# Experts of 128 slots with rounded weights become experts of 96 slots in f32, on four column quarters of TensorE

## The chip, the cores and the metric

The kernel runs on one core of a Trainium2 chip. The metric is the device time of one execution in microseconds, the median of several. The profile is one more execution; all its times are counted from the start of its span.

## The reference

One inference step of a decoder layer: a recurrent branch and an attention branch, merged and projected, and then a mixture of experts over 520 tokens (512 of the prompt, 8 of the samples). The change is in the mixture:

```python
D_MODEL = 1024; N_EXPERTS = 32; TOP_K = 4; D_FF = D_MODEL
logits = (t @ router_w).astype(jnp.float32) + router_b
top_v, top_e = lax.top_k(logits, TOP_K)
gate = jax.nn.softmax(top_v, axis=-1)
# for each expert e, for the tokens that chose it:
#   up = t @ w_up[e] + b_up[e]            (1024 -> 2048: a gate half and a linear half)
#   h  = clamped SwiGLU of the two halves (limit 7)
#   y += gate * (h @ w_down[e] + b_down[e])
```

An expert's weights are 1024 x 2048 and 1024 x 1024 f32 numbers: 12 MB, of which each number is used once for each of the 65 tokens (520 x 4 / 32) that an expert has on average. All 32 experts are read from HBM: 402.7 MB.

## The kernel before, in words

Up to about 650 us the kernel computes the branches, the projection and the router. The experts follow; they are sorted by their token counts, so that those with few tokens take the small places in a fixed pattern of places. The loops have a fixed number of steps and each place has a fixed number of slots (rows): 128 in 21 places and 64 (`FEW`) in 11. Places 0 and 1 have 128; then `triple` runs nine times with one place of 64 and two of 128; then `pair` and a last place of 64.

Weights come in 12 pieces of 1 MB for each expert: chunks 0 to 3 are the up matrix (512 columns each), 4 and 5 the down matrix, each in two halves. SyncE issues them (L612) into a ring in SBUF that holds 12 pieces, one expert. A piece is issued when the semaphore `half_used` says that the piece that lay there has been used, and TensorE counts `half_used` up behind the last matmul of each half.

A place of 128 slots (`block_of`) multiplies with f32 numbers split into two rounded parts (fp32r): for each product there are three matmuls, high x high, high x low, low x high. ScalarE makes the high part of each weight piece (`high_half`, L1846, a copy from the ring into one of six buffers `WH`), VectorE makes the low part (`low_half`, L2631, a subtraction in place in the ring), and both are needed before TensorE may start on the piece (L1350 up, L1367 down). Rows and hidden values are split the same way (L1888, L2707, L1896, L2726).

A place of 64 slots (`few_block`) multiplies in plain f32, straight from the ring, with nothing for ScalarE and VectorE to split. Its 64 rows use half of the array's columns, so each product is two matmuls side by side, one on columns 0 to 63 and one on columns 64 to 127, each with half of the 512 weight columns (L1403; in the down matrix L1418, of 512 of the 1024 columns each). Each f32 matmul of the program that is no transpose stands in the trace as two MATMUL and two LDWEIGHTS records (704 such products in `few_up` are the 1408 records of L1403); a rounded one and a transpose as one of each.

Around that, GpSimd gathers the rows of the next place (L2923) and adds the finished rows to the output in HBM (L2933), both with indirect DMAs; TensorE transposes the gathered rows (L1296, L1303) and the hidden values (L1315, L1411) by matmuls with the identity; biases are bf16 matmuls (L1319, L1396); ScalarE applies the gelu (L1892, L1940) and scales the results (L1935, L1963); VectorE clamps and multiplies (L2719, L2722, L2772, L2775).

## Time and profile before

| | |
|---|---|
| median of 3 runs | 1739.96 us (1731.2 to 1741.41) |
| span of the profiled execution | 1731.7 us |
| TensorE matmuls busy | 1665.8 us, 96% |
| VectorE busy | 1137.0 us, 66% |
| ScalarE busy | 888.9 us, 51% |
| read from HBM, written | 488.10 MB, 25.35 MB |

The profile's page divides the span into 40 slices of 43.3 us; each digit is the busy share of the slice in tenths. PE is TensorE's matmuls, PEld its weight loads, DVE VectorE, ACT ScalarE, POOL GpSimd, SP SyncE; "SPq" and "ACTq" are the queues of instructions of these engines. In a row of the timeline the columns are start, length, engine, line, operation, output<-input, shapes, and the count of merged instructions; in brackets stands idle time before them and what ended it.

### The profile page before, as it was taken

To read this page: it belongs to the slowest core of one execution; us is meant where nothing else is said; L and a number is where in the kernel's file an instruction comes from. 1 tells how busy PE (TensorE), PEld (TensorE's weight loads), DVE (VectorE), ACT (ScalarE), POOL (GpSimd) and SP (SyncE) were. 2 spreads that over 40 slices of the span, in tenths; PEclk is the share of its full clock that TensorE was granted. 3 is DMA by queue.
4 is the path that set the end of the run, shared out by engine and by line. 5 is a ranking of instruction groups with operands and counts; after the bars stand their busy time and mean duration, and the time that the engine had idled before them with its cause. 6 is when DMAs were issued, how large, how long until landed. Compare 5 with 4: busy or idle time off the path is not lost.

```text
span 1731.7 us, 27748 instructions
## 1 busy us (share of the span) xinstructions
PE 1665.8 (96%) x10106; PEld 1295.3 (75%) x10106; DVE 1137.0 (66%) x1555; ACT 888.9 (51%) x1019; POOL 217.4 (13%) x260
## 2 busy tenths in 40 slices
PE   7999999999998999999999999999989999999998
PEld 4899988798777777767677686767768676776765
DVE  6866785655356868949385684939477593938661
ACT  5245655533423446647274664728375573727461
POOL 0022000003331033110001001001000101100100
PEclk9999999999999999999999999999999999999999
DMA  5063233114437329999999999999999999999996
GB/s 219 30 215 120 84 123 101 46 62 134 140 107 261 104 71 403 348 396 402 398 405 378 409 386 398 394 399 399 384 410 383 400 397 403 395 395 409 381 399 231
DMA packets 100436, 498.74 MB, mean 288 GB/s; under 512 B 16350, under 2 KB 33846, under 8 KB 49648
## 3 DMA queue, kind: packets, MB, share of 16 engines
q1 hardware_dynamic: 84288, 458.39, 67.3%
q0 software_dynamic: 15920, 38.71, 7.9%
q8 instruction: 50, 0.82, 0.2%
q10 hardware_dynamic: 144, 0.55, 0.1%
q14 instruction: 34, 0.28, 0.0%
HBM read 488.10 MB, written 25.35 MB: 297 GB/s over the span
## 4 chain that ended last, share of the span: by engine, by line
PE 73%; DMA 14%; DVE 7%; issue 3%; ACT 2%; POOL 0%; ACTq 0%; SPq 0%; DVEq 0%; POOLq 0%
DMA ring<-in_w_exp 13%; PE bank L1350 13%; PE bank L1367 12%; PE bank L1403 9%; PE bank L795 7%; PE bank L695 5%; PE bank L850 5%; PE bank L1418 4%; PE bank L722 3%; PE bank L1114 2%; DVE ring_rounded L2631 1%; PE bank L662 1%; PE bank L863 1%; PE bank L884 1%; PE bank L872 1%
## 5 line engine op out<-in xcount | busy, mean ns | idle before, releaser
L2631 DVE TENSOR_TENSOR ring_rounded<-ring,wide_rounded 128x2048 fp32r<-128x2048 f32 x126 | 283.7, 2285 | 21.5 <-ACT wide_rounded L1846 21.3
L1846 ACT ACTIVATE wide_rounded<-ring 128x2048 fp32r<-128x2048 f32 x126 | 236.6, 1912 | 86.4 <-DMA ring<-in_w_exp 72.6
L1350 PE MATMUL bank<-ring_rounded,slab_rounded 128*128 128x512 f32 x672 | 264.3, 394 | 0.0
L1350 PE MATMUL bank<-xn_rounded,slab_rounded 128*128 128x512 f32 x672 | 224.9, 407 | 1.2 <-DVE ring_rounded L2631 0.8
L2631 DVE TENSOR_TENSOR ring_rounded<-ring,xn_rounded 128x2048 fp32r<-128x2048 f32 x84 | 190.2, 2285 | 20.6 <-ACT xn_rounded L1846 19.2
L1367 PE MATMUL bank<-wide_rounded,slab_rounded 128*128 128x512 f32 x504 | 172.4, 403 | 9.3 <-DVE slab_rounded L2726 8.9
L1846 ACT ACTIVATE xn_rounded<-ring 128x2048 fp32r<-128x2048 f32 x84 | 159.5, 1909 | 22.8 <-DMA ring<-in_w_exp 19.3
L2772 DVE TENSOR_SCALAR slab<-bank 128x256 f32<-128x256 f32 x22 | 9.3, 424 | 237.6 <-PE bank L1403 237.6
L1350 PE MATMUL bank<-wide_rounded,slab_rounded 128*128 128x512 f32 x504 | 159.0, 390 | 0.0
L1403 PE MATMUL bank<-ring,slab 128*64 128x256 f32 x1408 | 156.2, 380 | 0.0
L1350 PEld LDWEIGHTS bank<-xn_rounded,slab_rounded 128*128 128x128 f32 x672 | 130.0, 193 | 33.5 <-ACT xn_rounded L1846 3.4
L795 PE MATMUL bank<-ring_rounded 128*128 128x260 f32 x768 | 147.7, 291 | 0.0
L1350 PEld LDWEIGHTS bank<-ring_rounded,slab_rounded 128*128 128x128 f32 x672 | 128.2, 191 | 26.0
L2933 POOL DMA_INDIRECT out_y<-slab,small x32 | 58.5, 1828 | 674.2 <-ACT slab L1935 364.0
L1403 PEld LDWEIGHTS bank<-ring,slab 128*64 128x64 f32 x1408 | 98.1, 137 | 51.2 <-issue 1.9
L1367 PE MATMUL bank<-ring_rounded,slab_rounded 128*128 128x512 f32 x336 | 131.7, 392 | 0.0
L795 PEld LDWEIGHTS bank<-ring_rounded 128*128 128x128 f32 x768 | 117.8, 188 | 14.0 <-issue 11.9
L1367 PEld LDWEIGHTS bank<-wide_rounded,slab_rounded 128*128 128x128 f32 x504 | 95.3, 189 | 32.8 <-issue 13.2
L1350 PEld LDWEIGHTS bank<-wide_rounded,slab_rounded 128*128 128x128 f32 x504 | 94.7, 188 | 19.5
L2631 DVE TENSOR_TENSOR ring_rounded<-ring,qT_rounded 128x2048 fp32r<-128x2048 f32 x42 | 95.9, 2283 | 0.0
L695 PE MATMUL bank<-ring_rounded 128*128 128x260 f32 x512 | 93.6, 285 | 0.8 <-ACT wide L1534 0.8
L1846 ACT ACTIVATE qT_rounded<-ring 128x2048 fp32r<-128x2048 f32 x42 | 80.3, 1912 | 2.3 <-DMA out_y<-slab 2.3
(553 smaller groups left out, 2988.2 us busy)
## 6 DMA issues: line engine op xcount, KB each, us to landing
ring<-in_w_exp SPq DMA_DIRECT2D x384, 1024.0 KB, 14.0
ring<-in_w_blk SPq DMA_DIRECT2D x40, 512.0 KB, 3.3
slab<-in_w_tok SPq DMA_DIRECT2D x4, 1304.0 KB, 15.0
ring<-in_w SPq DMA_DIRECT2D x8, 512.0 KB, 3.3
ring<-in_w_out SPq DMA_DIRECT2D x2, 2048.0 KB, 15.5
xn<-in_xT SPq DMA_DIRECT2D x4, 520.0 KB, 7.9
ring<-in_k_cmp SPq DMA_DIRECT2D x32, 64.0 KB, 3.5
ring<-in_k_cmp POOLq DMA_DIRECT2D x32, 64.0 KB, 2.6
```

What stands on the lines that cost most here:

```text
L695: r = mm(bank[:, banks + h, 0:HN], w[:, k, wcols], a[:, k, cols], start=first and x == 0, stop=last and x == 2)
L722: r = mm(out, u[:, k, q], w[:, k, a:b], start=k == 0 and x == 0, stop=k == KD - 1 and x == 2)
L795: r = mm(bank[:, 6 + h, 0:HN], w[:, k, :], a[:, k, cols], start=k == 0 and y == 0, stop=k == KD - 1 and y == 2)
L850: r = mm(bank[:, 4 * h + 2 * f + x, :].rearrange("p (g c) -> p g c", g=NPAGES), w[:, f, x, :], a, start=l == 0 and y == 0, stop=l == LP - ...
L1114: return mm(out, three[0][x][k][:, a:a + n], w[:, k, :], start=first, stop=last)
L1350: r = mm(bank[:, c, :], a[:, 4 * h + k, :], w[:, k, :], start=False, stop=h == 1 and i == 11)
L1367: r = mm(bank[:, 4 + y, :], a[:, k, :], w[:, f, cols], start=k == 0 and x == 0, stop=k == KD - 1 and x == 2)
L1403: r = mm(bank[FEW * h:FEW * h + FEW, c, 0:256], XF[:, k, :], w[:, k, 256 * h:256 * h + 256], start=False, stop=k == KD - 1)
L1418: r = mm(bank[FEW * y:FEW * y + FEW, 4, :], HF[:, 2 * (c - 4) + k % 2, k // 2, :], w[:, k, y * 512:(y + 1) * 512], start=c == 4 and k == 0 ...
L1846: fn(WH[(2 * c + h) % 6], ring[:, half_of(c, h)], ACT.Copy).then_inc(S["wh_ready"], 1)
L2631: v.tensor_tensor(ring_r[:, half_of(c, h)], ring[:, half_of(c, h)], WHf[(2 * c + h) % 6], ALU.subtract)\
L2933: pool.indirect_dma_start(out=d["y"][:, :], out_offset=bass.IndirectOffsetOnAxis(ap=index, axis=0), in_=rows, in_offset=None, bounds_check ...
```

## The change

All places now work in plain f32. There are three kinds: 96 slots (`MID`, 20 places), 64 slots (`FEW`, 11 places, as before, save that the down matrix goes by 512 columns too), and one of 128 slots (`WIDE_AT`, place 14). The order of the places is written out as a list; the loop body is a group of six places, run twice, then the wide place, then the group twice again, then five places by themselves. A place of 96 slots has its three groups of 32 rows on three quarters of the array's columns, each with weight columns 0 to 383; the fourth quarter does weight columns 384 to 511 for all three groups, one after the other.

The splitting instructions of ScalarE and VectorE and their buffers are gone, and with them the semaphores `wh_ready`, `wl_ready`, `xl_ready` and `hl_ready`. TensorE waits for each 1 MB piece by itself (`piece_in`). The order of the pieces of the down matrix is (4,0), (5,0), (4,1), (5,1), and in HBM each of them is four blocks of 128 rows by 512 columns. VectorE gets one more small copy for each place (the gates of the rows that stand in the fourth quarter, or in the upper half), and ScalarE scales a place of 96 slots with eight instructions in place of one. The rows of the next place are transposed behind the first hidden part, before the down matrix.

```diff
-FEW = 64
-TRIPLES = 9
+FEW, MID = 64, 96
+GROUP = (MID, FEW, MID, MID, FEW, MID)
+BEFORE, BEHIND = 2, 2
+WIDE_AT = 2 + len(GROUP) * BEFORE
+LAST = (MID, FEW, MID, FEW, FEW)
+CAP = (MID, MID) + GROUP * BEFORE + (P,) + GROUP * BEHIND + LAST
...
+        PIECE_ORDER = [(c, h) for c in range(4) for h in range(2)] + [(4, 0), (5, 0), (4, 1), (5, 1)]
...
+            def product(c, slots, rows, w, first, last):
+                if slots == P:
+                    return mm(bank[:, c, :], rows(0, P), w, start=first, stop=last)
+                if slots == FEW:
+                    for y in range(2):
+                        r = mm(bank[64 * y:64 * y + 64, c, 0:256], rows(0, 64), w[:, 256 * y:256 * y + 256], start=first, stop=last)
+                    return r
+                for g in range(3):
+                    mm(bank[32 * g:32 * g + 32, c, 0:384], rows(32 * g, 32), w[:, 0:384], start=first, stop=last)
+                for g in range(3):
+                    r = mm(bank[96:128, c, P * g:P * (g + 1)], rows(32 * g, 32), w[:, 384:512],
+                           start=first and g == 0, stop=last and g == 2)
+                return r
...
+            def up_half(n, c, h, slots):
+                pe.wait_ge(piece_in[2 * c + h], 16 * n + 32)
+                w = weights(c, h)
+                for k in range(4):
+                    r = product(c, slots, lambda a, m: XT[:, 4 * h + k, a:a + m], w[:, k, :], False, h + k == 4)
+                r.then_inc(S["half_used"], 1)
...
+            def down(n, slots, meanwhile=None):
+                turn_hidden(n, slots, 0)
+                if meanwhile is not None:
+                    meanwhile()
+                pe.wait_ge(S["y_scaled"], n + 1)
+                pe.wait_ge(S["hh_ready"], 2 * n + 1)
+                down_half(n, 4, 0, slots)
+                turn_hidden(n, slots, 1)
+                down_half(n, 5, 0, slots)
                 pe.wait_ge(S["hh_ready"], 2 * n + 2)
+                down_half(n, 4, 1, slots)
+                down_half(n, 5, 1, slots)
...
-                fn(WH[(2 * c + h) % 6], ring[:, half_of(c, h)], ACT.Copy).then_inc(S["wh_ready"], 1)
...
-                v.tensor_tensor(ring_r[:, half_of(c, h)], ring[:, half_of(c, h)], WHf[(2 * c + h) % 6], ALU.subtract)\
-                    .then_inc(S["wl_ready"], 1)
```

On TensorE, at the start of the second place of `triple` before (chunk 0 of 128 slots): the biases and the first products, each row a run of equal matmuls with the shape of its output.

```order
L1319 MATMUL bank<-oT,kT 128x512 x4
L1339 ISA
L1350 MATMUL bank<-xn_rounded,slab_rounded 128x512
L1350 MATMUL bank<-ring_rounded,slab_rounded 128x512
L1350 MATMUL bank<-xn_rounded,slab_rounded 128x512 x2
L1350 MATMUL bank<-ring_rounded,slab_rounded 128x512
```

On TensorE now, in the first place of the group of six (96 slots): the end of the up matrix, the transposes, and the start of the down matrix.

```order
L1323 MATMUL bank<-ring,slab 32x384 x3
L1325 MATMUL bank<-ring,slab 32x128 x3
L1377 REGISTER_ALU
L1379 MATMUL bank<-ident,slab 128x128 x3
L1309 REGISTER_ALU
L1312 MATMUL bank<-ident,slab 128x128
L1312 MATMUL bank<-ident,slab 128x64 x7
L1343 REGISTER_ALU
L1323 MATMUL bank<-ring,slab 32x384 x3
L1325 MATMUL bank<-ring,slab 32x128 x3
```

Where three matmuls of 512 columns on the whole array stood for one block of 128 weight rows, six f32 matmuls on quarters stand now, 48 times six for each place.

On VectorE, in a place of 128 slots before: two of the subtractions stand between the hidden values' instructions, and a place has twelve.

```order
L2631 TENSOR_TENSOR ring_rounded<-ring,wide_rounded 128x2048
L2726 TENSOR_TENSOR slab_rounded<-bank,slab_rounded 128x512
L2631 TENSOR_TENSOR ring_rounded<-ring,wide_rounded 128x2048
L2718 REGISTER_ALU
L2719 TENSOR_SCALAR slab<-bank 128x512
L2720 REGISTER_ALU
L2722 SCALAR_TENSOR_TENSOR slab<-slab 128x512
```

On VectorE now, a place of 96 slots whole, behind the copies for the place before it:

```order
L2597 CAST kT<-small 96x128
L2589 COPY small<-small 128x1
L2594 COPY qT<-qT 32x3
L2602 TENSOR_SCALAR slab<-bank 128x384
L2605 SCALAR_TENSOR_TENSOR slab<-slab 128x384
```

The subtractions are gone, and only the hidden values' instructions and three small copies are left.

## Rows read from the trace of the kernel before

**Rows 1.** The page: busy time, then 40 slices; in it TensorE, DMA share, GB/s
```profile
PE 1665.8 (96%) x10106; PEld 1295.3 (75%) x10106; DVE 1137.0 (66%) x1555; ACT 888.9 (51%) x1019; POOL 217.4 (13%) x260
PE   7999999999998999999999999999989999999998
DMA  5063233114437329999999999999999999999996
GB/s 219 30 215 120 84 123 101 46 62 134 140 107 261 104 71 403 348 396 402 398 405 378 409 386 398 394 399 399 384 410 383 400 397 403 395 395 409 381 399 231
```

**Rows 2.** Stretches: length, engines' busy time (count), clock, DMA share, GB/s
```profile
843.70:943.00 99.30, 96.61 (x512) 71.27 (x510) 66.01 (x48) 56.42 (x44) 9.53 (x6) 0.98 1.00 396
700.00:740.00 40.00, 39.75 (x187) 32.10 (x186) 37.30 (x33) 25.33 (x18) 4.83 (x2) 1.00 0.93 341
906.00:961.00 55.00, 55.00 (x329) 40.87 (x329) 28.63 (x25) 22.17 (x21) 5.62 (x4) 1.00 0.98 383
961.00:976.00 15.00, 14.74 (x67) 9.01 (x64) 11.40 (x6) 12.62 (x9) 1.95 (x2) 1.00 1.02 425
1702.00:1717.00 15.00, 15.00 (x142) 9.53 (x140) 1.13 (x4) 2.20 (x4) 1.56 (x1) 1.00 0.70 262
```

**Rows 3.** DMA queues from 850 to 1640 us: packets, MB, share of 16 engines
```profile
q0 software_dynamic: 5888, 13.04, 6.5%
q14 instruction: 1, 0.01, 0.0%
```

**Rows 4.** SyncE's queue: who it waited for, in total, times, longest
```profile
SPq L612 <- PE bank L1350: 421.5, 168, 14.1
```

**Rows 5.** The page's groups: the splitting of one kind of piece
```profile
L2631 DVE TENSOR_TENSOR ring_rounded<-ring,wide_rounded 128x2048 fp32r<-128x2048 f32 x126 | 283.7, 2285 | 21.5 <-ACT wide_rounded L1846 21.3
L1846 ACT ACTIVATE wide_rounded<-ring 128x2048 fp32r<-128x2048 f32 x126 | 236.6, 1912 | 86.4 <-DMA ring<-in_w_exp 72.6
```

**Rows 6.** Timeline of TensorE, one place of 64 slots
```profile
843.51 0.63 PE L1396 MATMUL bank<-oT,kT 96*64 96x256 bf16 x8
843.97 10.53 PE L1403 MATMUL bank<-ring,slab 128*64 128x256 f32 x96
...
860.39 1.04 PE L1296 MATMUL bank<-ident,slab 128*128 128x128 f32 x8
...
866.66 1.04 PE L1319 MATMUL bank<-oT,kT 96*128 96x512 bf16 x4
```

**Rows 7.** Timeline of TensorE: f32 matmuls of 32 rows on four quarters
```profile
522.95 3.64 PE L996 MATMUL bank<-ring,wide 128*32 128x512 f32 x32
...
542.09 1.95 PE L1080 MATMUL bank<-slab,kT 128*32 128x128 f32 x64
543.86 2.58 PE L1080 MATMUL bank<-ring,kT 128*32 128x128 f32 x88
548.69 1.51 PE L1080 MATMUL bank<-ring,kT 128*32 128x128 f32 x40 [2.24 <-issue]
```

**Rows 8.** DMA queue of TensorE's code, in 0 to 520 us
```profile
q8 instruction: 28, 0.46, 0.4%
```

**Rows 9.** The same stretch, as a row of stretches
```profile
0.00:520.00 520.00, 503.42 (x3521) 433.48 (x3522) 334.69 (x764) 235.62 (x451) 76.19 (x147) 1.00 0.35 115
```

**Rows 10.** DMA queues in 541 to 546 us, then in 546 to 549 us
```profile
q1 hardware_dynamic: 137, 1.98, 93.1%
...
q8 instruction: 1, 0.02, 2.2%
```

**Rows 11.** Timeline of the end: last piece issued, last matmuls, scaling, last add
```profile
1702.01 0.33 SPq L612 DMA_DIRECT2D ring<-in_w_exp  x1
...
1718.75 5.37 PE L1418 MATMUL bank<-ring,slab 128*64 128x512 f32 x24
...
1724.25 1.38 ACT L1963 ACTIVATE slab<-bank,small 64x512 f32<-64x512 f32 x2 [5.01 <-PE bank L1418]
1726.53 1.44 POOL L2933 DMA_INDIRECT out_y<-slab,small  x1 [20.78 <-ACT slab L1963]
```

**Rows 12.** Pieces issued after 1690 us, from issue to landing
```profile
DMA to landing us min/median/max: 11.1/14.6/15.3
```

More of the change, by code:

```diff
@@ L196, in build @@
         eslot = [0, 1, 2, 4, 3, 5]
-        ebase = [16 * loads[s] for s in eslot]
         def chunk(name, n=1):
@@ new lines, in block_of, with groups @@
+            def block_of(n, b, slots, following, by_column=True):
+                gated(n, slots, 0)
+                gated(n, slots, 1)
+                hidden_copied(n, slots, 0)
+                if following:
+                    turned_rows(n + 1, following)
+                hidden_copied(n, slots, 1)
+                scaled(n, b, slots, by_column)
+            def groups(count, first, following):
+                with act.Fori(0, count) as t:
+                    for i, slots in enumerate(GROUP):
+                        block_of(len(GROUP) * t + (first + i), (first + i) % 2, slots, (GROUP + (following,))[i + 1])
@@ L2801, in _, with groups @@
+            def groups(count, first):
+                with dve.Fori(0, count) as t:
+                    for i, slots in enumerate(GROUP):
+                        block_of(len(GROUP) * t + (first + i), (first + i) % 2, slots, True)
             pick_expert(0, pick_two)
@@ L2803, in _ @@
             places(RT - 1)
-            low_rows(0)
             gate_low(RT - 1)
```

581 lines of the change are left out of this document (187 added, 394 removed).

## The prediction

> **What bounds the kernel now.** I read the page's slices first [rows 1]. TensorE is at 9 tenths almost everywhere, and from slice 16 (650 us) on the DMA engines are at 9 tenths too, at some 395 GB/s. So the 1060 us of experts have two candidates. The stretches tell them apart [rows 2]. One triple (two places of 128 slots, one of 64) lasts 99.3 us, 33.1 us an expert; TensorE's matmuls are busy 96.6 of it and the DMA share is 1.00. Inside it the load is uneven: right behind the place of 64 slots (961 to 976 us) the engines move 425 GB/s, and through the second place of 128 slots and the one of 64 (906 to 961 us) 383 GB/s at a share of 0.98, with TensorE busy all 55 us and SyncE's queue waiting for it to give pieces back: 421.5 us in 168 waits for L1350 alone [rows 4]. Each bounds in turn: TensorE while it is on large places, the DMA behind a small one.
>
> At 425 GB/s a piece of 1.049 MB takes 2.47 us, twelve take 29.6 us. The indirect gathers and adds take 6.5% of the engines [rows 3], 2.15 us of 33.1. With some code packets beside them (2.2% of 3 us x 16 engines is 1.06 us of one engine each [rows 10], five for an expert 0.3 us) the DMA floor is 32.1 us an expert, 1.0 us under today's pace. That 1.0 us is what a TensorE with slack can free; how fast it is beyond that does not matter.
>
> VectorE (66 of 99.3 us) and ScalarE (56) have slack already, so the work that goes away there, 12 subtractions of 2.285 us and 12 copies of 1.912 us for each large place [rows 5], is worth only the waits that it causes: the 2.7 us of a triple in which TensorE is not busy.
>
> **The change, part by part.** *A place of 96 slots.* Its shape is not in the trace, its parts are: on four quarters at once 32 records of 128x512 take 3.64 us with a last one of 0.59 us unhidden in part, 8 rounds of 0.43 us; and of 128x128, 88 records take 2.58 us, 22 rounds of 0.109 us [rows 7]. So four quarters do run side by side in f32, and a round costs its columns. For one block of 128 weight rows, three quarters have two records of 384 columns, 2 x 0.32 = 0.64 us, the fourth has six of 128, 6 x 0.109 = 0.656 us. The larger counts: 48 x 0.656 = 31.5 us. Biases: four banks of 0.16 us. Transposes: 6 hidden and 8 of rows at about 0.11 us (8 take 1.04 with the tail [rows 6]), 1.5 us. Six switches between whole and quartered array at 0.1 to 0.2 us, 1 us. Sum 34.7 us. Bounds: 33.5 us if the fourth quarter costs no more than the others, 40 us if its six loads leave gaps of a sixth.
>
> *A place of 64 slots.* Its products are the same matmuls in halves of 256 columns; it lasted 23.2 us (843.5 to 866.7) [rows 6]. I keep that.
>
> *The wide place.* 48 products of 512 columns at two records of 0.43 us [rows 7], 41.2 us, with the rest 44. It costs its neighbours 44 - 32 = 12 us at most, once; the small place three before it and the ring's twelve pieces hide part. I take 5 us.
>
> *Per three experts* TensorE then needs 2 x 34.7 + 23.2 = 92.6 us, against 96.3 us at the DMA floor. It keeps 3.7 us of slack, so the DMA sets the pace. Two large places in a row need 69.4 us where the DMA would give 64.2; the ring (12 pieces) covers the 5.2 us. I take 32.4 us an expert, a little above the floor, because there will be such pairs. From 740 to 1700 us are 29 experts: 29 x (33.1 - 32.4) = -20 us, bounds 0 and -29; with the wide place -15.
>
> *The start.* Expert 0's pieces come at the same events of the router. In 700 to 740 us the DMA share is 0.93 [rows 2], since TensorE gave pieces back late, behind the first splits: -3 us, bounds 0 and -8.
>
> *The end.* The last piece is issued at 1702.0 us, because a large place held it [rows 11], and lands at the latest 15.3 us later [rows 12]; from 1702 to 1717 us the share is 0.70 [rows 2]. With pieces free early the engines stay full: -4.5 us. From 1717.3 us to TensorE's last matmul, 1724.1 us, are 6.8 us of work on pieces that lie there; a TensorE that waits for pieces has only the last one to do, four blocks of four records in pairs, 8 rounds of 10.53 / 48 = 0.219 us [rows 6], 1.75 us: -5 us. Scaling and the add behind it stay (7.6 us), bounds 0 and -10 for both.
>
> *Waits that are new.* TensorE waits for `piece_in` with the next matmuls queued behind it; that is the DMA's pace, priced above. It waits for `hh_ready` behind the transposes of the first hidden part; the eight row transposes stand between (8 x 0.109 = 0.87 us), and ScalarE's copy of 384 columns is shorter than the 512 columns that it scales in 1.38 / 2 = 0.69 us [rows 11]. ScalarE's eight scalings, 2.5 us by estimate (eight at under half of 0.69), are waited for at the next place's down matrix, 22 us later. Cover everywhere; without it 1 us a place.
>
> *Code.* In 0 to 520 us TensorE ran 3521 matmuls and 3522 loads [rows 9] and its code queue brought 28 packets of 16 KB [rows 8]: one packet for 251 instructions. In 850 to 1640 us, eight triples, it brought none [rows 3]: the loop body, some 1000 instructions, stays where it was read. The new body is four places of about 1230 (288 x 4 and 76) and two of 420, 5760 instructions; I count on it being read again all the time, one packet for 128 matmuls, which last 128/12 x 0.656 = 7.0 us. The trace has one place where code was late: the fast run of L1080 stops after 64 + 88 matmuls for 2.24 us with nothing awaited [rows 7], and the packet came in 546 to 549 us, not while the DMA was 93% busy before [rows 10]. 128 matmuls back is the 24th of the first run, at 542.8 us; the stop ends at 548.7. So a packet was usable 5.9 us after the one before it was entered, under a nearly full DMA. 5.9 is under 7.0: hidden, with 1.1 us to spare.
>
> By the Trainium skill (Runtime: NRT & Kernel Launch, Instruction fetch mechanics), TensorE's instruction memory holds 2048 instructions and is refilled in blocks of 256 while the current block runs. The trace agrees with the block (251) and with a body of 1000 that stays; that 5760 do not stay is that page's word, no row of this kernel shows it.
>
> **Sum.** -15 - 3 - 4.5 - 5 = -27.5 us. The profiled execution's 1731.7 us becomes 1704; it lies 8.3 us under the median of the runs, and on that scale 1740 - 27.5 = 1712 us, -1.6%.
>
> **Rivals.** *1. Code arrives too late (slower).* If a packet takes 9 us instead of 5.9 (the DMA share here is 1.02, not 0.93), a large place takes 1230/256 x 9 = 43 us, three experts 109.6 us, 36.5 an expert: 29 x 3.4 = +99, less some 7 of start and end, 1832 us. It decides from 7.9 us a packet: then a large place takes 38.1 and three experts 99.3 as now. For it: one late packet in a busy stretch. Against: if TensorE falls back, fewer pieces are in flight and packets come sooner, which pulls towards 8.5 us, 1786 us. 23%.
>
> *2. It comes out even.* Packets of 7.5 to 8 us, or a fourth quarter with gaps, so that a large place takes 36.5 to 38 us: the pace stays 33 us, only part of the ends is gained, 1723 to 1757 us. 20%.
>
> *3. The quarters do not overlap when unequal.* If the fourth quarter's six records ran behind the others instead of beside them, a block would take 1.3 us, a large place 65 us: 20 x 30 = +600 us, 2300 us. Against: no round of four in rows 7 costs more than its columns, though all are equal there. 3%.
>
> *4. Records cost a fixed time.* Twelve records for a block leave 55 ns each. In rows 7 88 records take 2.58 us, 27 ns each after the tail, so 12 need 0.33 us at least and the block's 0.656 is not touched. Were a whole load and matmul paid in turn, 2 x 27 = 54 ns for each record, it would still be 0.65 us. Only at a cost of 62 ns or more would it bind: 0.74 us a block, a large place 38.9 us, three experts 101 us, +16 - 7, 1749 us. 2%.
>
> By the Trainium skill (TensorE: Matmul & The Clock Gate, Wait — 56ns, not 53.3ns?) a matmul can cost about 62 ns in the sequencer. By the 27 ns of rows 7 this trace denies it.
>
> **Numbers.** The forecast, DMA-bound at 32.1 to 32.9 us an expert, gives 1690 to 1722 us: 52%. Faster by over 1% (1% is about what a measurement of this kernel can tell from no change; under 1722.6) 0.52, within 1% 0.20, slower 0.28 (rivals 1, 3, 4). Range: down to 1692 (all of the pace, 29, and all of the ends), up to 1786 (rival 1 at 8.5 us).
>
> **What would show it.** Right: a group of six places of about 194 us at 425 GB/s outside the gathers; TensorE idle in short waits for pieces, in small places above all; 0.66 us for each block in a large place; code packets every 7 us in large places and no idle time there marked "issue"; the last matmul less than 3 us behind the last landing. Wrong: idle time of TensorE of 1 to 3 us each 128 matmuls with landed pieces in the ring; DMA share under 0.97 in the pace; blocks of over 0.75 us.

## The result, and the profile of the changed kernel

The changed kernel takes 1747.32 us (median of 4, 1745.54 to 1754.53) against 1736.55 us of the kernel before (1731.20 to 1741.41): a ratio of 1.0078, with a 95% interval of 1.0045 to 1.0111. It is slower by 0.8%, where 1.6% faster was forecast. The profiled execution's span is 1744.4 us, 12.7 more than 1731.7.

The page: busy time of the engines, and three of the rows of 40 slices, as in [rows 1].

```profile
PE 1652.3 (95%) x19416; PEld 1401.3 (80%) x19416; DVE 521.3 (30%) x1271; ACT 466.1 (27%) x930; POOL 194.1 (11%) x263
PE   7999999999999999999998998999998899999896
DMA  5064233124547239999999999999999999999995
GB/s 215 32 218 119 79 123 109 37 66 128 145 124 269 69 112 394 361 378 389 405 393 402 397 398 405 398 372 371 392 403 390 384 374 404 387 405 400 390 410 230
```

VectorE fell from 1137 to 521 us and ScalarE from 889 to 466, as the edit says. The bytes per microsecond hardly moved (393 GB/s against 396 from 850 to 1640 us): the splitting went away and the DMA engines deliver what they delivered.

Stretches, with the columns of [rows 2]: about the first and the second round of the first group of six places, the place of 128 slots, 33 us behind the second jump back, and the last pieces.

```profile
740.00:940.00 200.00, 193.05 (x3056) 172.32 (x3060) 14.47 (x42) 36.39 (x79) 17.12 (x14) 0.99 1.01 395
940.00:1138.00 198.00, 187.14 (x2857) 163.43 (x2850) 14.47 (x42) 30.93 (x66) 12.25 (x10) 0.99 1.01 398
1138.00:1182.00 44.00, 43.93 (x121) 20.06 (x123) 2.96 (x6) 5.54 (x10) 2.44 (x2) 1.00 0.98 368
1378.00:1411.00 33.00, 30.43 (x467) 28.14 (x467) 2.59 (x7) 2.07 (x4) 0.48 (x1) 0.82 0.95 361
1711.00:1735.00 24.00, 18.52 (x152) 10.34 (x148) 1.92 (x6) 1.66 (x5) 0.00 (x0) 1.00 0.57 227
```

TensorE now has slack (187 of 198 us), the DMA share is 1.01, and 395 to 398 GB/s is within 1% of the 396 GB/s of the triple in [rows 2]. The DMA queues from 850 to 1640 us, as in [rows 3]:

```profile
q1 hardware_dynamic: 40636, 295.92, 93.4%
q0 software_dynamic: 4862, 12.93, 6.7%
q8 instruction: 89, 1.46, 0.7%
```

And the same stretch's row of weights in the kernel before:

```profile
q1 hardware_dynamic: 41191, 299.94, 94.4%
```

In the same 790 us 4 MB of weights fewer arrive than before, and 1.46 MB of code do arrive, where there was none. From the start of place 1 to that of place 31 (found by the bf16 bias matmuls) the kernel before takes 989.7 us, the changed one 993.7. Counted by the DMA instead (an expert has landed when the last of its 1536 weight packets of 8 KB has ended), the landings of experts 1 to 30 span 963.6 us before and 977.4 now, and the last expert takes 41.0 us more, 36.0 before. Places in which TensorE does not wait are as forecast: 34.1 to 34.4 us for 96 slots, 23.1 for 64, 44.0 for 128.

The inside of a place of 96 slots, as in [rows 7]: one block of 128 weight rows is two such pairs of rows.

```profile
740.72 0.50 PE L1323 MATMUL bank<-ring,slab 128*32 128x384 f32 x3
740.74 0.49 PE L1325 MATMUL bank<-ring,slab 128*32 128x128 f32 x3
741.04 0.50 PE L1323 MATMUL bank<-ring,slab 128*32 128x384 f32 x3
741.07 0.49 PE L1325 MATMUL bank<-ring,slab 128*32 128x128 f32 x3
```

The three quarters' records start every 0.32 us and the fourth's run beside them: 0.65 us a block, with 0.656 in the sum. What TensorE waited for in 740 to 1700 us (total, times, longest):

```profile
PE bank L1320 <- DMA ring<-in_w_exp: 23.1, 19, 3.2
PE bank L1323 <- issue: 13.0, 4, 5.4
PE bank L1323 <- DMA ring<-in_w_exp: 10.2, 8, 2.2
```

The waits for pieces stand above all in the small places (L1320), as forecast. The waits marked "issue" are read as late code. The two long ones, 5.43 and 5.33 us, stand where each loop begins its second round, and e6, which has no jump back, has none. The first is

```profile
938.41 0.51 PE L1323 MATMUL bank<-oT,kT 96*32 96x384 bf16 x3 [5.43 <-issue]
```

The pieces' way from issue to landing, before and now, on the two pages:

```profile
ring<-in_w_exp SPq DMA_DIRECT2D x384, 1024.0 KB, 14.0
```

```profile
ring<-in_w_exp SPq DMA_DIRECT2D x384, 1024.0 KB, 25.4
```

TensorE gives pieces back sooner, and they stand in the queue longer: more is asked of the DMA engines, and they deliver no more. At the end the last weight packet ends at 1734.7 us (before: 1717.0), and from there to the end of the span are 9.7 us (before: 14.7).

### The profile page after: what moved, and what is told of

Same layout as the page of the kernel before. It is cut to its first block, busy times and chain, and to the rows that moved or that the text cites. A ratio compares the mean times of both kernels' runs of the same rounds, so it can differ in the third digit from the quotient of the medians.

```text
span 1744.4 us, 44915 instructions
## 1 busy us (share of the span) xinstructions
PE 1652.3 (95%) x19416; PEld 1401.3 (80%) x19416; DVE 521.3 (30%) x1271; ACT 466.1 (27%) x930; POOL 194.1 (11%) x263
## 4 chain that ended last, share of the span: by engine, by line
PE 70%; DMA 20%; DVE 5%; issue 2%; SPq 2%; ACT 1%; POOL 0%; DVEq 0%; POOLq 0%; ACTq 0%
PE bank L1325 18%; DMA ring<-in_w_exp 17%; PE bank L1323 11%; PE bank L1320 7%; PE bank L808 7%; PE bank L708 5%; PE bank L863 5%; PE bank L735 3%; PE bank L1317 2%; PE bank L1127 2%; SPq L623 2%; PE bank L876 1%; PE bank L675 1%; PE bank L1379 1%; PE bank L897 1%
## 5 line engine op out<-in xcount | busy, mean ns | idle before, releaser
L1323 PE MATMUL bank<-ring,slab 128*32 128x384 f32 x5760 | 643.4, 492 | 14.8 <-DMA ring<-in_w_exp 10.2
L1325 PE MATMUL bank<-ring,slab 128*32 128x128 f32 x5760 | 651.1, 275 | 0.0
L1325 PEld LDWEIGHTS bank<-ring,slab 128*32 128x32 f32 x5760 | 628.5, 111 | 1.9
L1320 PE MATMUL bank<-ring,slab 128*64 128x256 f32 x2112 | 244.0, 384 | 30.4 <-DMA ring<-in_w_exp 29.7
L1323 PEld LDWEIGHTS bank<-ring,slab 128*32 128x32 f32 x5760 | 226.5, 110 | 26.0 <-DMA ring<-in_w_exp 14.1
L1320 PEld LDWEIGHTS bank<-ring,slab 128*64 128x64 f32 x2112 | 147.1, 138 | 117.0 <-DMA ring<-in_w_exp 41.0
L1834 ACT ACTIVATE slab<-bank 128x384 f32<-128x384 f32 (+2 forms) x64 | 29.3, 457 | 457.6 <-PE bank L1325 327.0
L808 PEld LDWEIGHTS bank<-ring_rounded 128*128 128x128 f32 x768 | 117.8, 188 | 14.1 <-issue 12.0
L1838 ACT ACTIVATE slab<-bank 128x384 f32<-128x384 f32 (+2 forms) x64 | 29.2, 457 | 246.2 <-PE bank L1379 246.2
L1847 ACT ACTIVATE slab<-bank,small 96x384 f32<-96x384 f32 (+2 forms) x64 | 34.7, 543 | 175.8 <-PE bank L1325 116.2
L708 PEld LDWEIGHTS bank<-ring_rounded 128*128 128x128 f32 x512 | 79.2, 188 | 1.4 <-issue 1.0
L708 PE MATMUL bank<-xn_rounded,ring_rounded 128*128 128x260 f32 x256 | 72.3, 282 | 0.0
L808 PE MATMUL bank<-xn_rounded,ring_rounded 128*128 128x260 f32 x256 | 72.2, 282 | 0.0
L1939 DVE TENSOR_TENSOR ring_rounded<-ring,ring_rounded 128x1024 fp32r<-128x1024 f32 x40 | 48.8, 1224 | 2.4 <-ACT ring_rounded L1470 1.7
L708 PEld LDWEIGHTS bank<-xn_rounded,ring_rounded 128*128 128x128 f32 x256 | 48.2, 188 | 0.0
L808 PEld LDWEIGHTS bank<-xn_rounded,ring_rounded 128*128 128x128 f32 x256 | 48.2, 188 | 0.0
```

Source lines behind the costliest of these rows:

```text
L708: r = mm(bank[:, banks + h, 0:HN], w[:, k, wcols], a[:, k, cols], start=first and x == 0, stop=last and x == 2)
L808: r = mm(bank[:, 6 + h, 0:HN], w[:, k, :], a[:, k, cols], start=k == 0 and y == 0, stop=k == KD - 1 and y == 2)
L1320: r = mm(bank[64 * y:64 * y + 64, c, 0:256], rows(0, 64), w[:, 256 * y:256 * y + 256], start=first, stop=last)
L1323: mm(bank[32 * g:32 * g + 32, c, 0:384], rows(32 * g, 32), w[:, 0:384], start=first, stop=last)
L1325: r = mm(bank[96:128, c, P * g:P * (g + 1)], rows(32 * g, 32), w[:, 384:512], start=first and g == 0, stop=last and g == 2)
L1939: v.tensor_tensor(ring_r[:, raw_blk[j % 4]], ring[:, raw_blk[j % 4]], ring_r[:, hi_blk[j % 3]].bitcast(F32), ALU.subtract)\
```

## The experiments

Each ratio is to the kernel before, run beside it on the same chip. The runs stand on several chips and in several rounds, where the median of the kernel before lay between 1732.1 and 1736.6 us, so between rounds the ratios are the better measure. "Place" and "pace" are counted as above. Some runs leave work out: e1, e2, e11 and e12 most rows of the adds (all but e11 of the gathers too), e7, e9 and e10 the experts' own rows, e3, e4 and e12 the rows beyond 64 of four experts. The others do the whole work.

| run | median, us | ratio (95%) |
|---|---|---|
| e1_after_two_rows | 1688.2 | 0.9741 (0.9725 to 0.9757) |
| e2_before_two_rows | 1685.7 | 0.9724 (0.9708 to 0.9740) |
| e3_pairs_flat | 1738.4 | 1.0029 (1.0009 to 1.0048) |
| e4_pairs_loop | 1729.8 | 0.9985 (0.9972 to 0.9998) |
| e5_no_wide | 1747.6 | 1.0091 (1.0070 to 1.0113) |
| e6_no_jump | 1743.7 | 1.0075 (1.0054 to 1.0096) |
| e7_even_rows | 1730.4 | 0.9983 (0.9968 to 0.9997) |
| e8_few_first | 1729.0 | 0.9971 (0.9957 to 0.9984) |
| e9_uneven_same_tokens | 1867.7 | 1.0746 (1.0704 to 1.0789) |
| e10_before_even_rows | 1720.9 | 0.9928 (0.9906 to 0.9951) |
| e11_after_adds_two_rows | 1701.8 | 0.9803 (0.9770 to 0.9836) |
| e12_pairs_two_rows | 1666.2 | 0.9605 (0.9572 to 0.9638) |
| e13_before_spread | 1736.0 | 1.0006 (0.9992 to 1.0021) |
| e14_after_spread | 1735.6 | 1.0006 (0.9993 to 1.0018) |
| e15_few_first_spread | 1717.4 | 0.9900 (0.9881 to 0.9919) |
| e16_pairs_first_spread | 1738.2 | 1.0018 (1.0004 to 1.0032) |
| e17_before_96_slots | 1727.2 | 0.9977 (0.9961 to 0.9993) |
| e18_pairs_first_shifted | 1720.2 | 0.9935 (0.9921 to 0.9948) |

### What sets the pace: the rows that are gathered and added (e1, e2, e11, e12)

```diff
-                    gather(GX[(n + 1) % 2][0:CAP[n + 1], :], rows_of(n + 1))
+                    m = CAP[n + 1] if n < 2 else 2
+                    gather(GX[(n + 1) % 2][0:m, :], rows_of(n + 1)[0:m])
...
+                if isinstance(n, int) and 1 <= n < NE - 1:
+                    rows, index = rows[0:2], index[0:2]
                 pool.indirect_dma_start(out=d["y"][:, :], ...
```

> The changed kernel, but from expert 3 on the indirect gather fetches 2 rows in place of 96 or 64, and from expert 1 to 30 the indirect add writes 2 rows in place of all: the other rows of these experts are left out of the output. Theory A (the 16 DMA engines set the pace in both kernels, and gathers and adds cost more than their own share because weight packets beside them take over 400 ns): the pace falls from 33.1 to 33.4 us an expert to what TensorE needs, 30.6 us (four places of 34.4 and two of 23.0), or to 12 pieces of packets of 309 to 314 ns, 29.8 to 30.3 us; about 31 us, 30 x 2.3 = 70 us less: 1677 us. Rival B (the pace is set by TensorE with its waits for code): it stays within 10 us of 1747. Rival C (the DMA sets it, but rows cost only their own share of 2.0 us an expert): 1690 us.

> The kernel before with the same edit (2 rows in each gather and add). Theory A (the DMA engines set the pace of 33.0 us before too, with TensorE right under it): the pace falls only to what TensorE needs with its inner waits, 96.6 / 3 = 32.2 us, so 20 to 25 us less, 1714 us; the DMA share falls to 0.95. Rival B (before, TensorE with its waits behind the splits set the pace): nothing changes, 1737 us.

The changed kernel falls by 59 us, the kernel before by 47 to 49. Stretches: one triple of e2, and of e1 two places behind each other (96 and 64 slots), then the next three with the jump.

```profile
844.70:938.80 94.10, 94.10 (x511) 70.42 (x511) 65.47 (x48) 55.85 (x43) 8.80 (x6) 1.00 1.00 402
```

```profile
845.80:903.30 57.50, 57.41 (x836) 48.13 (x832) 4.64 (x14) 10.82 (x24) 4.56 (x4) 1.00 1.01 410
903.30:1002.60 99.30, 94.04 (x1442) 83.19 (x1440) 7.23 (x21) 16.41 (x35) 6.83 (x6) 0.97 0.96 383
```

Without rows the triple of the kernel before is TensorE and nothing else: 94.1 us, 31.4 an expert. So the 99.3 us of [rows 2], with 96.6 us of matmuls, contained 5 us that went with the rows, part of it inside matmul records, and rival B falls: TensorE with its waits for splits did not set 33.1. Theory A was 11 us too low for e1, where late code at the jumps is bare (the last row, at a granted clock of 0.97 and with 94 of 99 us busy: the places on both sides of the jump took 39.6 and 36.7 us instead of 34.1 to 34.4), and 28 too high for e2, since it put TensorE's own need before at 32.2.

> The changed kernel with whole gathers, but adds of 2 rows for experts 1 to 30 (the other rows are left out of the output). Of the 59 us that both were worth, theory M (each row moved costs the same packet time, either way) gives half: 1718 us. Rival (an add reads and writes HBM and costs more than a gather): 1700 to 1708 us.

With whole gathers and adds of 2 rows: 1701.8 us, so the adds are worth 45 of the 59 us. An add costs three to four times a gather (45 against 14 us by the medians, 48 against 11 by the ratios). A row's packet of 4 KB takes 327 ns in an add, and in the median 191 ns in a gather (159 in the kernel before).

> e4_pairs_loop with gathers and adds of 2 rows, so neither rows nor code packets stand beside the weights, and TensorE needs only 28.7 us an expert. It measures the floor that the prediction worked out. As predicted there (12 pieces of 2.47 us): 29.6 us an expert in the loops, which with 3.1 us less than the 33.0 of e4_pairs_loop gives about 1730 - 30 x 3.1 = 1637 us. If weight packets keep the mean of 321 to 324 ns that they have beside rows too: 30.9 us an expert, 1670 us.

1666.2 us. Its stretches where TensorE is neither ahead nor behind:

```profile
1070.00:1130.00 60.00, 59.93 (x297) 31.53 (x294) 5.01 (x13) 7.65 (x14) 4.56 (x4) 1.00 1.01 421
```

From 786 to 1146 us two experts landed every 59.8 to 60.0 us: 29.9 to 30.0 an expert. The bare floor of the prediction, 12 x 2.47 = 29.6, holds within 0.3. Rows put more on it than 2.15 us. In places 4 to 13 an expert landed every 29.9 us here, every 32.4 in e4, the same kernel with its rows (2.4 us more), and every 33.0 in the kernel before (3.1 more). Behind 1146 us the pace of e12 falls to between 30 and 33 us, in the loop whose code is read again (below), and so the whole lies near the 1670 us of the second theory and not at 1637.

### Does a faster TensorE help, and what does code cost (e3, e4, e5, e6)

```diff
-GROUP = (MID, FEW, MID, MID, FEW, MID)
+GROUP = (MID, FEW) * 3        # e3; BEFORE, BEHIND stay 2
+GROUP = (MID, FEW)            # e4, with BEFORE, BEHIND = 6, 6
```

> The changed kernel with (96, 64) three times as its group of six: 16 places of 96, 15 of 64, one of 128. The few rows beyond 64 of the four experts that don't fit are left out. TensorE needs 28.7 us an expert instead of 30.6, the loop body has about 4950 instructions. Theory A (the DMA sets the pace): the pace stays 33.2 us, TensorE only waits more: 1740 to 1747 us. Rival B (TensorE with late code sets it): 24 x 1.9 = 45 us less, 1702 us.

> As e3_pairs_flat, the same places in the same order, but the group is (96, 64) and runs six times on either side of the wide place: the loop body has about 1650 instructions. Theory A: no code packets within the loops, 0.27 us of DMA time an expert less, 24 x 0.27 = 6.5 us less than e3_pairs_flat (3 to 8). Rival D (code fetching is hidden): equal to e3_pairs_flat within 2 us. Rival B (late code stalls TensorE and sets the pace): 20 us or more less.

With 1.9 us less of TensorE work an expert e3 has a pace of 32.9 us instead of the changed kernel's 33.1, and 9 us of the 45 that rival B asks for. The DMA sets the pace. e4 is 8.6 us faster than e3 with the same places, a little over the 3 to 8 of theory A. DMA queues in 850 to 1120 us, of e3 and then of e4:

```profile
q1 hardware_dynamic: 14250, 103.79, 94.7%
q0 software_dynamic: 1606, 4.10, 6.0%
q8 instruction: 28, 0.46, 0.7%
```

```profile
q1 hardware_dynamic: 14360, 104.57, 95.1%
q0 software_dynamic: 1743, 4.44, 6.5%
```

Code packets take 0.24 us of all 16 engines for each expert in e3 and 0.27 in the changed kernel, and where they are gone more weights pass. They were not hidden: 24 x 0.27 = 6.5 us of the 8.6 are their own time on the DMA engines. For the other 2 us there is no test.

```diff
-CAP = (MID, MID) + GROUP * BEFORE + (P,) + GROUP * BEHIND + LAST
+CAP = (MID, MID) + GROUP * BEFORE + (MID,) + GROUP * BEHIND + LAST      # e5
...
-GROUP = (MID, FEW, MID, MID, FEW, MID)
-BEFORE, BEHIND = 2, 2
+GROUP = (MID, FEW, MID, MID, FEW, MID) * 2                              # e6
+BEFORE, BEHIND = 1, 1
```

> The changed kernel with place 14 of 96 slots in place of 128: TensorE needs 34.4 us there instead of 44.0, and nothing is left out, since the largest expert has 89 rows. Theory A (the place of 128 holds the weight queue up as the prediction said, 5 us): 1742 us. Rival E (the ring covers it, as between 1115 and 1183 us of e4_pairs_loop, where two experts landed in 68.1 us with it and 66.3 us around it): 0 to 2 us less than 1747.

> The changed kernel with the same places in the same order, but the group of twelve places written out, each group run once: the same instructions are read, without a jump back. Theory F (in the changed kernel the two jumps back cost TensorE 5 to 7 us each, since code behind a jump isn't read ahead, and part of it comes back at the end): the places 7 and 20 last 34.4 us of work with no idle time of 5 us marked issue, and the whole takes 2 to 6 us less, 1741 to 1745 us. Rival G (the ring covers the stalls, or they are not the jumps): 1747 us, in the second case with the same stalls.

e5: no gain that can be measured, rival E. The stretch of the place itself shows why there was something to hope for: 368 GB/s at a share of 0.98 in the rows of 1138 to 1182 us above, and in e5

```profile
1138.00:1172.00 34.00, 34.00 (x619) 33.30 (x615) 2.60 (x7) 6.09 (x13) 2.44 (x2) 1.00 1.02 397
```

Around the jump of the second loop e5 moves less than the changed kernel, here in this order:

```profile
1350.00:1450.00 100.00, 92.44 (x1417) 80.75 (x1417) 7.26 (x21) 16.20 (x35) 7.35 (x6) 0.98 0.98 378
```

```profile
1350.00:1450.00 100.00, 92.38 (x1372) 80.35 (x1368) 5.94 (x18) 16.19 (x35) 7.32 (x6) 0.93 0.99 383
```

That may be where the gain went, but nothing tests it. The 5 us of the prediction for this place are not shown. e6: TensorE's waits in 740 to 1700 us are these two, and the ones marked "issue" are gone:

```profile
PE bank L1320 <- DMA ring<-in_w_exp: 33.2, 26, 3.0
PE bank L1323 <- DMA ring<-in_w_exp: 15.5, 15, 2.2
```

So the long stalls are the jumps back. Their price is 3.6 us by the medians, but e6 ran in another round: by the ratios (1.0075 against 1.0078) it is 0.5 us, and the intervals overlap. What two jumps cost the whole kernel is below what these rounds can tell.

### Rows that go to few engines (e7, e9, e10, e13, e14, e17)

```diff
+                if 2 <= n < NE - 1:
+                    return entall[0:FEW, WIDE_AT, 0:1].bitcast(U32)      # e7; e10 the same in the kernel before
                 return entall[0:CAP[n], n, 0:1].bitcast(U32)
```

> The changed kernel, but the gathers and adds of experts 2 to 30 all move exactly 64 rows, those of the expert in place 14, in place of 43 to 89 rows of their own; their own rows are left out of the output. The number of rows is nearly the same (64 against 65 on average), but each of 16 engines gets 4 of every 64. Theory H (rows go to the engines in turn, so the first engines get more of them, 145 against 115 of 2080 for each direction, fall behind up to 17 us by the end, and the last pieces land late): in the last 30 us before the last landing an engine is idle 2 us on average instead of 9.8, and the whole takes 6 to 8 us less, 1740 us. Rival I (the spread at the end comes from code packets or from the deep queue): 9 to 10 us idle as before, 1746 us.

> As e7_even_rows (all gathers and adds of experts 2 to 30 take the tokens of place 14; the experts' own rows are left out), but each moves as many rows as its expert has, 43 to 89, in place of 64. There are 3% more rows than in e7_even_rows, worth 2 us at 59 us for all. Theory H (what made e7_even_rows 17 us faster than the changed kernel is that 64 rows go evenly to 16 engines): 1744 us, with 9 us idle before the last landing. Rival J (it is that always the same tokens, near in HBM, are moved, or the descriptors of empty slots that are gone): 1732 us, as e7_even_rows and 2 us.

> The kernel before with 64 rows of one expert in all gathers and adds of experts 2 to 30 (their own rows are left out). Theory K (uneven rows cost the changed kernel alone, whose queue of pieces is full, so that engines drift apart): 2 to 4 us less than before, 1730 us. Rival L (they cost any kernel that the DMA paces): 12 to 17 us less, 1718 us.

e7 is 17 us faster than the changed kernel, more than either theory said, and the idle time at its end is 6.2 us, where H said 2 and I 9 to 10: H is right that evenness matters, and wrong on where. e10 is 13 us faster than the kernel before: rival L, any kernel that the DMA paces pays for it. Some of both is that 64 rows are fewer than the 70 that an expert of the later places has. From the DMA records of the trace, 750 to 1650 us, the weight packets of 8 KB that took 700 ns or more (their median is 309 to 313 ns), and in 1200 to 1640 us the engine time for each expert:

```
                          700 ns, more  weights  rows  code   an expert landed every
before                    448 of 41700  31.25    2.24  0.00   33.25 us
changed                   294           31.19    2.30  0.27   33.56
e10_before_even_rows        6           30.78    2.26  0.01   32.65
e13_before_spread         450           31.20    2.22  0.00   33.19
e17_before_96_slots        84           31.02    2.42  0.00   33.06
e14_after_spread          173           31.01    2.43  0.28   33.33
e15_few_first_spread       55           30.75    2.19  0.00   32.53
```

The long packets stand in bunches: in the kernel before 4, 4, 8 and 6 that start within 0.5 us of each other at 906.3, 909.5, 912.5 and 916.0 us, 621 to 1421 ns long, about as far apart as TensorE gives pieces back in a place of 128 slots (35.5 / 12 = 3.0 us). I read them as engines that have run ahead and wait for the next piece: a DMA share of 1.00 contained idle time. That TensorE alone held the pieces back is ruled out by e10, where its work is the same and 6 of 448 are left. e9 told nothing of its question. It changed the packets themselves: with 43 to 89 rows exactly, the software queue in 860 to 1000 us is the first row here, that of the changed kernel the second:

```profile
q0 software_dynamic: 4933, 1.73, 6.8%
```

```profile
q0 software_dynamic: 832, 2.03, 5.9%
```

six times the packets for fewer bytes, and 120 us more. From 800 to 1600 us its gathers took 34.3 us in the median from issue to landing (11.0 in the changed kernel) and its adds 20.1 (9.0), up to 67. Of 416 row packets in 860 to 1000 us, 357 ran with at most three others beside them. By the Trainium skill (DMA: Bandwidth & Descriptors, Why a DMA increments its semaphore by 16 and not by 1) the number of engines is the largest one up to 16 that divides the rows, so that 67 rows stay on one; the few packets at a time agree.

So e13, e14 and e17 keep every row and token and change only the slot: an expert's r-th row goes to block r mod 16 of the slots.

```diff
+                        here = slots_in.rearrange("e (s x) -> e s x", x=2)[:, 0:slots, x].rearrange("e (b a) -> e a b", a=16)
+                        r = v.tensor_copy(spread[slots, x].rearrange("e (a b) -> e a b", a=16), here if x else here.bitcast(I32))
```

> The kernel before with all rows, but an expert's rows are laid out over its slots so that its r-th row stands in block r mod 16 of 8 (or 4) slots; they used to fill the slots from 0 on. Theory N (16 engines take the slots of an indirect DMA in 16 blocks, so that of an expert's rows in 128 slots the first 8 engines move 8 each and the last 7 none; these engines run ahead and then wait): the packets of over 700 ns, 448 of 41700 between 750 and 1650 us, are gone, and the time falls by 10 to 13 us as in e10_before_even_rows, 1722 us. Rival J (that run was faster because it moves always the same tokens): 1734 us.

> The changed kernel with all rows and the same layout, blocks of 6 or 4 slots. Theory N: 12 to 15 us less than the changed kernel, 1733 us, as e7_even_rows less the 3% of rows that it left out. With e13 it says what the change itself is worth when no kernel has rows on few engines: 8 to 12 us slower, from code packets and late code, since both are then nearer to what TensorE needs but still paced by the DMA. Rival J: 1747 us.

> The kernel before with all rows, but the gathers and adds of its places of 128 slots cover 96 slots, laid out in blocks of 6 as in e14 (the largest expert has 89 rows). e13 showed that in 128 slots the layout changes nothing: 8 engines end within 0.9 us, 8 after 4.7 us, whichever slots hold rows. Theory O (the number of slots of a row DMA decides how evenly 65 to 89 rows go to 16 engines, in the changed kernel too): the packets of over 700 ns fall from 450 to under 200 and the time by 8 to 12 us, 1725 us. Rival P (the kernel before is held by its own large places, where TensorE has 35.5 us of work, so evener rows buy nothing; e10 gained by the 3% of rows left out and by its 64 slots): 1733 us.

e14 is 12 us faster than the changed kernel (1.0006 against 1.0078) with all its rows: that rows went to few engines cost it that, and rival J falls there. But the forecast that e14 would be 8 to 12 us slower than e13 did not come true, they are equal. e17 is 0.2% faster than the kernel before, with 84 long packets instead of 448: theory O in direction, half of its price. Its gain stands in the early places, where an expert has 60 rows on average: in places 4 to 13 an expert landed every 32.4 us, 33.0 in the kernel before, in places 17 to 29, with 71 rows, every 33.0 against 33.2.

e17 and e14 move the same rows in the same layout, and but for places 0, 1 and 14 their row DMAs have the same slots. So the pair is the fairest measure of the change itself: e14, with the new matmuls, is 0.3% slower (1.0006 against 0.9977, the intervals touch).

e13 changed nothing, and its packets say why. In a gather of 128 slots with 67 rows the empty slots' packets of 4 bytes follow each other every 6 ns on one engine. The records name no engine, but which packets follow each other on one can be worked out from their ends and starts. In the kernel before 8 engines move 8 rows each and end 4.7 to 5.1 us after the start, one moves 3, seven none. In e13 again 8 engines have 8 rows each, three have one, five none. By the Trainium skill (DMA: Bandwidth & Descriptors, The descriptor swizzle) the engine of a partition p in a transfer of 128 is 8 x (p >> 6) + ((p >> 2) & 7); with my layout, where the slots with p mod 8 under 4 are full, this gives 8 engines with 8 rows, three with one and five with none, and for the layout of before 8, one with 3, and 7. The trace agrees in both: a gather of 68 rows at 1041 us in the kernel before has eight engines with 8 rows and one with 4; one of 71 rows at 1241 us in e13 has eight with 8 and four with 2, 2, 2 and 1, as the formula gives for 71. So e13 took the rows from one half of the engines to another. A layout that follows this rule was not tried, and what the kernel before would gain by it is open; e10 bounds it by 13 us.

### Versions that may beat both (e8, e15, e16, e18)

```diff
+LOOPED = 10                                   # e8, e15
+FIRST = (FEW, FEW) + 8 * (MID,)
+LAST = (MID, FEW)
+CAP = FIRST + GROUP * LOOPED + LAST           # GROUP = (MID, FEW)
...
+CAP = (FEW, FEW) + GROUP * 5 + 8 * (MID,) + GROUP * 5 + LAST      # e16, e18
...
+            for _ in range(160):              # e18 alone
+                pe.wait_ge(S["small_in"], 16)
```

> A version with all rows: places 0 and 1 have 64 slots (the experts there have 62 and 53 rows), then eight places of 96 written out, then (96, 64) ten times in a loop of some 1650 instructions, then (96, 64); no place of 128. TensorE needs 29.8 us an expert on average, there are code packets only in the first ten places and the last. Theory A: the pace is the DMA's, 33.0 us, the tail is that of e4_pairs_loop: 1727 to 1731 us, 0.2% under the kernel before. If the first places, where the ring is full, are worth more with 64 slots: 2 us less still. Rival: eight places of 96 in a row at 34.4 us with late code hold the DMA up: 1735 to 1740 us.

> e8_few_first with that layout, all rows. Theory N: 12 to 15 us less than its 1729, 1715 us. But the eight places of 96 in a row need 34.4 us each where the DMA would give about 32.2, so part may be held back: 1718 us. Rival J: 1729 us.

> As e15, but with the eight places of 96 in the middle: (64, 64), (96, 64) five times in a loop, eight of 96, (96, 64) five times in a loop, (96, 64). TensorE, which waits in the pairs, falls behind by 8 x 2.2 = 18 us in the middle while the ring has pieces to fetch, and makes it up behind: 2 to 4 us less than e15, 1713 us. If the ring does not cover it, 1 to 3 us more than e15.

> e16_pairs_first_spread with 160 waits that are already met, 80 instructions, at the very start of TensorE's program; nothing else. In e16 both loops of 1675 instructions were read again in every round and TensorE stood 5 us at each jump; the same body was kept in e8, e15 and the first loop of e4. Counted in TensorE's compiled program, the bodies that were kept start at 211, 9 and 17 past a multiple of 256, the ones read again at 147 and 160, the one read again in part at 76. Theory Q (a body is kept where it lies in 7 blocks of 256 instructions and not where it touches 8): with the start at 226 and 239 both loops are kept, no code packets in them, and the time is 1714 us, 1 to 4 us under e15. Rival R (what keeps it is something else, as the order of the places): 1738 us as e16.

e15 is the fastest: 1717.4 us, 1.0% under the kernel before and 1.8% under the changed one by the ratios. Against e17, whose row DMAs are as even, it is 0.8% faster: with less code read and 64 slots in the first places the new matmuls do beat the old ones, and how much of that is TensorE's slack was not tested apart. e8 to e15 is the layout of rows alone, 12 us. e16, the same places in another order, is 21 us slower. TensorE's waits in 740 to 1700 us, of e16 and then of e18:

```profile
PE bank L1327 <- issue: 45.1, 12, 4.4
PE bank L1329 <- issue: 16.2, 4, 4.4
```

```profile
PE bank L1325 <- DMA ring<-in_w_exp: 37.7, 38, 2.6
PE bank L1328 <- DMA ring<-in_w_exp: 15.9, 17, 2.0
```

and the DMA queues in 1410 to 1650 us, the same loop in both:

```profile
q1 hardware_dynamic: 12249, 89.18, 93.9%
q0 software_dynamic: 1269, 3.77, 6.3%
q8 instruction: 31, 0.51, 0.8%
```

```profile
q1 hardware_dynamic: 12722, 92.65, 94.7%
q0 software_dynamic: 1344, 4.06, 7.0%
```

80 instructions ahead of everything else take 61 us of "issue" and all code packets out of the loops, and with them 18 us by the medians, 14 by the ratios. What theory Q forecast for the code came true and R falls: it is not the order of the places. Where a body is read again TensorE stands at every jump and DMA time goes to code. The count of blocks in Q does not come out of its own figures, though: 1675 instructions from 211 past a multiple of 256 on reach into an eighth block (211 + 1675 = 1886, seven blocks are 1792), and that body was kept, and from 76 on they lie in seven, and that one was partly read again. And e4 and e12 have the same program on TensorE: in 1200 to 1640 us 32 code packets came in e4, 60 in e12. So the start of the body matters, but a rule for it stays open. That e18 would beat e15 by its order did not come true; it is 3 us slower by the medians, 6 by the ratios.

By the Trainium skill (Runtime: NRT & Kernel Launch, Instruction fetch mechanics) a taken branch out of the blocks that are held forces a fetch before execution goes on. The "issue" rows of the changed kernel, e6, e16 and e18 agree: long stalls at jumps into code that was read again, none without.

## Why the prediction was wrong

**What bounds the kernel: wrong in its reading.** The step that failed is "1.0 us under today's pace. That 1.0 us is what a TensorE with slack can free". TensorE did not hold the pace: its old work goes through at 31.4 us an expert once the rows are away (e2), and 1.9 us less of the new work gave 0.2 (e3). The floor was put together as 29.6 us of pieces and 2.15 us of rows at their own share. The first term was nearly right (29.9 in e12). The second was 3.1 us in the kernel before, for two reasons that a share does not show: beside rows, more weight packets take 400 to 550 ns (a quarter of those beside row packets in the changed kernel and 6% in the kernel before, 1% elsewhere), and rows lie on few engines, so that the others run ahead and wait, inside packets that count as busy. 29.9 + 3.1 = 33.0, today's pace. In row DMAs of 96 and 64 slots the second term was 2.4 us (e4, places 4 to 13). The forecast pace of 32.4 was reached there, in e4 and also in e17 with TensorE's old work: the row DMAs had set the rest, not TensorE. The changed kernel has those slots too, but with code came to 32.9 in places 4 to 13 and 33.6 in 17 to 29. The 383 GB/s in 906 to 961 us of [rows 2] at a share of 0.98 were taken as TensorE's; with the long packets at 906 to 930 us I now put them down to those waits. The mistake could have been seen: a share of 1.00 over the whole triple left a faster TensorE nothing to free.

**Places.** 34.7, 23.2 and 44 us were forecast; 34.1 to 34.4, 23.0 and 44.0 came. Rivals 3 and 4 fell with the first block.

**Pace: -15 forecast, +4.0 came** between the starts of places 1 and 31, +13.8 between the landings of experts 1 and 30. That there was no gain is the floor. Code packets cost 0.27 us an expert, about 8 in all, and the term was in the floor with 0.3; new is that the kernel before pays none of it and had nothing idle to pay it from. Rows in 96 slots instead of 128 probably gave some back (294 long packets instead of 448; in the kernel before e17 got 4 to 5 us from it). The two jumps and the place of 128 slots could not be told from nothing.

**The start: -3 forecast.** Place 1 starts at 712.5 us and at 712.1 before, so nothing.

**The end: half right.** The step from the last landing to the end was -5 and is -5.0 (14.7 to 9.7), with the last matmul 2.4 us behind the last landing. But the -4.5 for evener engines behind 1702 us came out the other way: in the last 30 us before the last landing an engine is idle 9.8 us on average, 4.1 before, probably since with TensorE fast and the ring all in the queue the engines with fewer rows had run further ahead. With rows at 2 of each expert it is 1.2 us in e1 and 0.9 in e2, so it is the rows; but with 64 even rows it is still 6.2 (e7), so uneven rows are only part of it. The stretch of 1711 to 1735 us above shows it: a share of 0.57.

**Code.** "I count on it being read again all the time, one packet for 128 matmuls": right, 158 packets in the whole kernel and 50 before. "Hidden, with 1.1 us to spare": right for TensorE in straight code: e6, without a jump back, has no "issue" row. It failed in two ways that the sum did not have. A jump back is not straight code: 5 us at each. And the packets' own time on the DMA engines, priced within a floor that was thought to have slack, was paid. Rival 1 had the direction of the result and not its size: at 9 us a packet it asked for 1832 us. The result lies in rival 2, "it comes out even", by its time, but with a mechanism that stands in none of the four: TensorE was not held up, the DMA engines were full already. None of the three signs for "wrong" came, as all of them watched for a TensorE or DMA engines with too little to do.

**Sum.** Forecast -27.5 us; the spans say +12.7: start +0.4, pace +4.0, and the last place from 29.9 to 38.2 us, +8.3, in which it waits for the last pieces. By the landings: expert 1 lands 1.0 us earlier, the 29 that follow take 13.8 us longer, the last one 5.0 us longer, and what stands behind it is 5.0 us shorter.

## What to carry to other kernels

Where the DMA share is 1.00, do not count on a faster compute engine until the same bytes have been seen moving faster over a whole period: the best stretch of a period is not its floor, because rows that are gathered and added elsewhere in it cost more than their share. Look at how many rows each DMA engine gets, and at weight packets of two to four times the usual length, which are engines that wait. And look for code packets inside a loop whose body should stay: shifting the whole program by 80 instructions was worth 14 to 18 us here.

## What the runs showed of the hardware

- A gather of 128 slots with 67 rows is done on 8 engines with 8 rows each and one with 3; seven have none. Gathers of exactly the 43 to 89 rows of an expert landed 34.3 us after their issue in the median, adds 20.1, instead of 11.0 and 9.0 with 96 or 64 slots.
- An indirect add cost three to four times an indirect gather of the same rows (45 and 14 us in 30 experts each, by the medians); a row's packet of 4 KB took 327 ns in an add, 159 to 191 in the median in a gather.
- On TensorE a loop body of 1675 instructions was kept when it began 211, 226, 239, 9 and 17 past a multiple of 256, read again each round at 147 and 160, and at 76 in some rounds, more of them in e12 than in e4. The starts are counted in the compiled program; the traces show the code packets alone. Jumps into code that was read again cost TensorE 4.4 to 6.2 us at the longest beside full DMA engines, and the granted clock was 0.82 in the 33 us behind the second one of the changed kernel.
- A code packet of 16 KB took 1.05 us of one DMA engine in the mean.
- A weight packet of 8 KB takes 309 to 313 ns in the median and 320 to 326 in the mean; taking away VectorE's and ScalarE's splitting did not shorten it (31.25 against 31.19 us an expert).
